# Gathering the first expert groups from unscaled residual rows, with weights in the place of the scaled rows

## What is computed

```python
h = h + mix(rms_norm(h, norm) @ w_in) @ w_out
hf = rms_norm(h, m_norm[layer])
g_idx = argmax(hf @ w_group + b_group)            # one of 4 groups
top_val, top_idx = top_k(e_logits_of_group, 2)    # two of its 8 experts
combine = one_hot(expert_idx) * softmax(top_val) * g_prob
for e in range(32):
    hid = silu(hf @ w_gate[e]) * (hf @ w_up[e])   # 1024 -> 256
    h += (hid @ w_down[e]) * combine[:, e:e + 1]  # 256 -> 1024
```

## Time and profile before

| | before |
|---|---|
| time, median of 3 runs | 781.3 us (780.98 to 781.67) |
| profiled execution, first to last instruction | 778.7 us |
| TensorE matmul busy | 718.9 us (92%) |
| TensorE weight load busy | 459.4 us (59%) |
| DVE busy | 324.4 us (42%) |
| ScalarE busy | 205.9 us (26%) |
| read from HBM | 240.00 MB |
| bytes moved, mean rate | 242.14 MB, 311 GB/s |

### The profile page before, as it was taken

One profiled execution on the slowest core, in us unless ns is written; L12 is line 12 of the kernel. 1 busy time (PEld: TensorE's weight loads), 2 busy tenths in 40 slices (PEclk: granted clock), 3 DMA queues, 4 the chain that ended last, 5 costly groups with the idle time before them and its releaser, 6 DMA issues.

```text
span 778.7 us, 16693 instructions
## 1 busy us (share of the span) xinstructions
PE 718.9 (92%) x7444; PEld 459.4 (59%) x7444; DVE 324.4 (42%) x688; ACT 205.9 (26%) x414; POOL 31.7 (4%) x99
## 2 busy tenths in 40 slices
PE   9999999999989998999999999999998976786696
PEld 7778787658646464564548746884764543343342
DVE  7476977535353422333235065541445321221222
ACT  2574577215100000000041454630510000000003
POOL 7006000000000000000000000000000000000000
PEclk9999999999999997999999999999999998989999
DMA  8644113499999999999999731019999999999995
GB/s 265 201 107 142 56 57 112 161 418 417 386 420 419 420 421 421 417 419 422 411 339 370 231 107 58 2 36 424 421 391 421 422 420 419 421 422 422 420 406 199
DMA packets 72757, 242.14 MB, mean 311 GB/s; under 512 B 9894, under 2 KB 37660, under 8 KB 52588
## 3 DMA queue, kind: packets, MB, share of 16 engines
q1 hardware_dynamic: 72476, 240.52, 79.0%
q10 hardware_dynamic: 208, 0.54, 0.2%
HBM read 240.00 MB, written 1.05 MB: 310 GB/s over the span
## 4 chain that ended last, share of the span: by engine, by line
PE 60%; DMA 15%; DVE 4%; issue 1%; SPq 1%; ACT 0%; ACTq 0%
PE ps L1554 11%; PE ps L1874 10%; PE ps L1396 7%; PE ps L1497 6%; DMA M<-in_m_w_gate_dram 6%; PE ps L1630 5%; PE ps L1512 5%; DMA M<-in_m_w_up_dram 4%; DMA M<-in_m_w_down_dram 4%; PE ps L1035 2%; DVE H L2488 1%; PE ps L1411 1%; PE ps L1696 1%; PE ps L1768 1%; PE ps L1505 1%
## 5 line engine op out<-in xcount | busy, mean ns | idle before, releaser
L1554 PE MATMUL ps<-M 128*32 128x256 f32 x2016 | 124.2, 396 | 18.4 <-DMA M<-in_m_w_gate_dram 11.4
L1554 PEld LDWEIGHTS ps<-M 128*32 128x32 f32 x2016 | 66.7, 114 | 74.7 <-issue 16.9
L1089 PE MATMUL ps<-M 128*128 128x272 f32 x352 | 85.3, 397 | 0.1
L1874 PE MATMUL ps<-M 128*128 128x256 f32 (+2 forms) x288 | 79.9, 434 | 0.0
L1497 PEld LDWEIGHTS ps<-M 128*128 128x128 f32 x608 | 71.5, 192 | 12.3 <-issue 11.8
L1497 PE MATMUL ps<-M 128*128 128x128 f32 x608 | 76.9, 278 | 0.0
L1089 PEld LDWEIGHTS ps<-M 128*128 128x128 f32 x352 | 65.6, 190 | 15.4 <-issue 1.7
L1630 PE MATMUL ps<-M 128*32 128x512 f32 x448 | 58.7, 671 | 15.5 <-DMA M<-in_m_w_down_dram 15.5
L1512 PE MATMUL ps<-M 128*128 128x512 f32 (+1 forms) x120 | 62.8, 647 | 5.3 <-DVE H L2488 5.3
L1874 PEld LDWEIGHTS ps<-M 128*128 128x128 f32 x288 | 53.7, 190 | 22.6 <-issue 15.6
L2485 DVE TENSOR_TENSOR H<-H,ps 128x512 f32<-128x512 f32 x60 | 41.2, 687 | 57.5 <-PE ps L1512 57.3
(11 more groups left out here) (462 smaller groups left out, 843.6 us busy)
## 6 DMA issues: line engine op xcount, KB each, us to landing
M<-in_m_w_gate_dram SPq DMA_DIRECT2D x31, 2048.0 KB, 19.0
M<-in_m_w_down_dram SPq DMA_DIRECT2D x24, 2048.0 KB, 22.8
M<-in_m_w_up_dram SPq DMA_DIRECT2D x24, 2048.0 KB, 21.6
M<-in_o_w_in_dram SPq DMA_DIRECT2D x12, 1024.0 KB, 9.5
M<-in_e_w_in_dram SPq DMA_DIRECT2D x11, 1024.0 KB, 6.7
M<-in_m_w_down_dram SPq DMA_DIRECT2D x10, 1024.0 KB, 18.1
M<-in_m_w_up_dram SPq DMA_DIRECT2D x9, 1024.0 KB, 17.9
M<-in_m_w_down_dram SPq DMA_DIRECT2D x4, 1536.0 KB, 13.3
```

The costliest lines, as they stand in the source:

```text
L1089: ins = pe.matmul(ps[:, n % 4, 0:T], wringE[:, (n // 2) % 4, k, (n % 2) * P:(n % 2) * P + P], (xnE if n else xuE)[:, k], start=(k == 0), s ...
L1554: ins = pe.matmul(ps[32 * e:32 * e + 32, 3 * x, 0:FF], xgT[q % 2][:, k, 32 * e:32 * e + 32], w, start=(k == 0), stop=(k == KD - 1))
L1874: ins = pe.matmul(ps[rows, unit % 4, 0:n], lhs(k), rhs(k), start=(k == 0), stop=(k == KD - 1))
```

## The change

- The two first gathers (q = 0 and q = 1) of layer 0 read the stationary operand straight from `H` (`rows_at`), with a step of eight floats. As these rows are not scaled, `rs` is multiplied into `R` instead: the one-hot matrix goes to `RW[q]`, and `R` is that times `rs`, one more DVE operation each time. `RW` is then weighted in place.
- `normed` is not called before the gather in layer 0, but after `half_done` 1 (tiles 0 and 2) and after the copy of `hidT` in quarter 0 (tile 1). The gather of quarter 2 waits for it, and so does the first `accumulated`, which changes `H`.
- `xn` (1.5 MB) holds the first halves of gate matrices 0 to 2 until then (`first_half`). Their place in slot 1 is free, and the second halves of up matrices 4 to 6 go there without waiting for `half_done`.
- 2 MB of quarter 0 (a down matrix and a half, half an up matrix) are issued after `y_done` 4 and `lru_in` 2, before the wait for `sa_evac`.
- The meta rows' sums in quarters 0 to 5 and in the spare pass of layer 0 are kept in strips: `combine` writes 32 rows in each group of 32 partitions, and one add of 128x256 puts all four pieces into `H[:, 2, 0:256]`. `strips_joined` brings them to the meta rows in quarter 6 (three copies, two adds); the sums of quarter 6 are added in the old form.
- Semaphore counts follow from this (`loaded`, `ld_half`).

```diff
@@ -287,6 +287,7 @@
+        first_half = [[xn[:, n].rearrange("p k t -> p (k t)") for n in range(3)], []]
@@ -357,22 +358,23 @@
-                def whole(u, src):
-                    j = UNIT_SLOT[y][u]
-                    for e in (0, 2):
-                        sp.dma_start(slots[j][:, e:e + 2, :], src[:, e:e + 2, :]).then_inc(s(f"ld_s{j}"), 16)
-                    sp.dma_start(apart[2], src[:, 2, 0:D]).then_inc(s(rest), 16)
+                    sp.wait_ge(s("y_done"), NTURN - 1)
+                    sp.wait_ge(s("lru_in"), 2)
+                    sp.dma_start(slots[3][:, 1, :], down[:, 1, :]).then_inc(s("ld_s3"), 16)
+                    sp.dma_start(slots[3][:, 2, 0:D], down[:, 2, 0:D]).then_inc(s("ld_s3"), 16)
+                    sp.dma_start(apart[2], up[:, 2, 0:D]).then_inc(s("ld_pv_ys"), 16)
-                    whole(2, down[:, 0:4])
+                    sp.dma_start(slots[3][:, 0, :], down[:, 0, :]).then_inc(s("ld_s3"), 16)
+                    sp.dma_start(slots[3][:, 2, D:2 * D], down[:, 2, D:2 * D]).then_inc(s("ld_s3"), 16)
+                    sp.dma_start(slots[3][:, 3, :], down[:, 3, :]).then_inc(s("ld_s3"), 16)
@@ -391,6 +393,10 @@
+                            sp.dma_start(slots[j][:, 0:3, D:2 * D], gate[:, 0:3, D:2 * D]).then_inc(s(f"ld_s{j}"), 16)
+                            sp.dma_start(slots[j][:, 3, :], gate[:, 3, :]).then_inc(s(f"ld_s{j}"), 16)
+                            sp.dma_start(xn.rearrange("p n k t -> p n (k t)"), gate[:, 0:3, 0:D]).then_inc(s(f"ld_s{j}"), 16)
+                            continue
@@ -419,9 +425,9 @@
+                            sp.dma_start(slots[j][:, 0:3, 0:D], up[:, 4:7, D:2 * D]).then_inc(s("ld_half"), 16)
-                            sp.dma_start(slots[j][:, 0:3, 0:D], up[:, 4:7, D:2 * D]).then_inc(s(f"ld_s{j}"), 16)
@@ -806,16 +812,16 @@
-                act.wait_ge(s("rec"), (5, 10)[y])
-                normed(0)
-                if nt == 3:
-                    normed(2)
+                if y == 1:
+                    act.wait_ge(s("rec"), (5, 10)[y])
+                    normed(0)
-                act.wait_ge(s("rec"), (6, 11)[y])
-                normed(1)
+                if y == 1:
+                    act.wait_ge(s("rec"), (6, 11)[y])
+                    normed(1)
@@ -825,6 +831,11 @@
+                    if q == 0 and y == 0:
+                        act.wait_ge(s("half_done"), 2 * y + 1)
+                        act.wait_ge(s("rec"), (6, 11)[y])
+                        normed(0)
+                        normed(2)
@@ -1404,11 +1417,14 @@
+            def rows_at(n, k):
+                return H[:, n, :].rearrange("p (d k) -> p k d", k=KD)[:, k, :]
-                        ins = pe.matmul(ps[:, GATHER_BANK[k // 2], (k % 2) * P:(k % 2) * P + P], xn[:, n, k, :], R[:, n, :],
+                        ins = pe.matmul(ps[:, GATHER_BANK[k // 2], (k % 2) * P:(k % 2) * P + P], rows_at(n, k) if y == 0 else xn[:, n, k, :], R[:, n, :],
...
@@ -1491,10 +1508,11 @@
-                def gather(done=None, ks=range(KD)):
+                def gather(done=None, ks=range(KD), first=False):
-                            ins = pe.matmul(ps[:, 1 + k // 4, (k % 4) * P:(k % 4) * P + P], xn[:, n, k, :], R[:, n, :],
+                            from_rows = rows_at(n, k) if first and y == 0 else xn[:, n, k, :]
+                            ins = pe.matmul(ps[:, 1 + k // 4, (k % 4) * P:(k % 4) * P + P], from_rows, R[:, n, :],
@@ -1511,8 +1529,7 @@
-                        ins = pe.matmul(ps[32 * g:32 * g + META, bank, 0:256], rt_[:, TOK[n]], ys[:, 256 * g:256 * g + 256],
-                                        start=True, stop=True)
+                        ins = pe.matmul(ps[QUAD[g], bank, 0:256], rt_[:, 0:32], ys[:, 256 * g:256 * g + 256], start=True, stop=True)
...
@@ -1549,6 +1571,8 @@
+                            elif u == 0 and k < KD // 2 and e < len(first_half[y]):
+                                w = first_half[y][e][:, FF * k:FF * k + FF]
@@ -1559,7 +1583,8 @@
-                pe.wait_ge(s("xn_set"), (3, 5)[y])
+                if y == 1:
+                    pe.wait_ge(s("xn_set"), (3, 5)[y])
...
@@ -1611,13 +1636,15 @@
-                        gather(ks=range(0, 2))
+                        if y == 0 and q == 1:
+                            pe.wait_ge(s("xn_set"), (3, 5)[y])
+                        gather(ks=range(0, 2), first=(q == 0))
-                        gather(s("g_done"), range(2, 4))
+                        gather(s("g_done"), range(2, 4), q == 0)
@@ -1630,7 +1657,7 @@
-                    gather(ks=range(4, KD)).then_inc(s("g_done"), 1)
+                    gather(ks=range(4, KD), first=(q == 0)).then_inc(s("g_done"), 1)
@@ -2402,9 +2429,14 @@
-                    return tt(R[:, t_].rearrange("p t (e c) -> p t e c", e=4),
-                              iota[:, 1:CAP + 1].unsqueeze(1).unsqueeze(1).to_broadcast([P, m, 4, CAP]),
-                              RM[:, t_, 0:4].unsqueeze(3).to_broadcast([P, m, 4, CAP]), ALU.is_equal).then_inc(s("R_set"), 1)
+                    if y == 1:
+                        return tt(R[:, t_].rearrange("p t (e c) -> p t e c", e=4),
+                                  iota[:, 1:CAP + 1].unsqueeze(1).unsqueeze(1).to_broadcast([P, m, 4, CAP]),
+                                  RM[:, t_, 0:4].unsqueeze(3).to_broadcast([P, m, 4, CAP]), ALU.is_equal).then_inc(s("R_set"), 1)
+                    link(tt(RW[0][:, t_].rearrange("p t (e c) -> p t e c", e=4),
+                            iota[:, 1:CAP + 1].unsqueeze(1).unsqueeze(1).to_broadcast([P, m, 4, CAP]),
+                            RM[:, t_, 0:4].unsqueeze(3).to_broadcast([P, m, 4, CAP]), ALU.is_equal))
+                    tt(R[:, t_], RW[0][:, t_], wide3(rs[:, ri], P, t_, m), ALU.mult).then_inc(s("R_set"), 1)
@@ -2452,12 +2484,17 @@
-                    tt(by_slot(R), iota[:, 1:CAP + 1].unsqueeze(1).unsqueeze(1).to_broadcast([P, nt, 4, CAP]),
-                       RM[:, t_, 4 * q:4 * q + 4].unsqueeze(3).to_broadcast([P, nt, 4, CAP]), ALU.is_equal).then_inc(s("R_set"), 1)
+                    hot = RW[q] if y == 0 and q == 1 else R
+                    made = tt(by_slot(hot), iota[:, 1:CAP + 1].unsqueeze(1).unsqueeze(1).to_broadcast([P, nt, 4, CAP]),
+                              RM[:, t_, 4 * q:4 * q + 4].unsqueeze(3).to_broadcast([P, nt, 4, CAP]), ALU.is_equal)
+                    if hot is not R:
+                        link(made)
+                        made = tt(R[:, t_], hot[:, t_], wide3(rs[:, ri], P), ALU.mult)
+                    made.then_inc(s("R_set"), 1)
-                    tt(by_slot(RW[q % 2]), by_slot(R), WT[:, t_, 4 * q:4 * q + 4].unsqueeze(3).to_broadcast([P, nt, 4, CAP]),
+                    tt(by_slot(RW[q % 2]), by_slot(RW[q] if y == 0 and q < 2 else R), WT[:, t_, 4 * q:4 * q + 4].unsqueeze(3).to_broadcast([P, nt, 4, CAP]),
@@ -2483,15 +2520,31 @@
-                    for g in range(4):
-                        c = slice(256 * g, 256 * g + 256)
-                        ins = tt(H[0:META, 2, c], H[0:META, 2, c], ps[32 * g:32 * g + META, 6 + j % 2, 0:256], ALU.add)
-                    return ins
+                    return tt(H[:, 2, 0:256], H[:, 2, 0:256], ps[:, 6 + j % 2, 0:256], ALU.add)
+                    if y == 0 and q == 0:
+                        v.wait_ge(s("xn_set"), (3, 5)[y])
+                        if y == 0 and j == 0 and q == NQ - 2:
+                            for g in range(4):
+                                c = slice(256 * g, 256 * g + 256)
+                                ins = tt(H[0:META, 2, c], H[0:META, 2, c], ps[32 * g:32 * g + META, 6, 0:256], ALU.add)
+                            ins.then_inc(s("acc"), 1)
+                            continue
+                def strips_joined():
+                    strip_rows = (at(36608, 2, 256), at(28800, 1, 256))
+                    v.wait_ge(s("acc"), acc0 + nu * (NQ - 2))
+                    for g in range(1, 4):
+                        last = v.tensor_copy(strip_rows[(g - 1) // 2][0:META, (g - 1) % 2], H[32 * g:32 * g + META, 2, 0:256])
+                    link(last)
+                    for x, c in zip(strip_rows, (slice(256, 768), slice(768, D))):
+                        last = tt(H[0:META, 2, c], H[0:META, 2, c], x[0:META].rearrange("p g c -> p (g c)"), ALU.add)
+                    link(last)
@@ -2539,6 +2592,8 @@
+                    if q == NQ - 2 and y == 0:
+                        strips_joined()
```

18 lines of the change are left out of this document (12 added, 6 removed).

## The result

The changed kernel takes 792.78 us, the median of its runs (792.37 to 793.58), beside 781.48 for the kernel before on the same chip: a ratio of 1.014, 95% interval 1.012 to 1.016. It is 11.3 us slower, where 5.6 was forecast. The profiled execution has a span of 791.1 us, 12.4 more than before, and at the last down product of the first expert stage TensorE is 12.16 us late already. So the whole loss lies ahead of that point.

What follows compares the result with a forecast made beforehand. TensorE and the transfers were taken to end the first expert stage together, with TensorE deciding after the change: +10.4 + 0.5 - 5.3 = +5.6 us on 781.3 gives 786.9 us. Range 777.9 to 789.2, likeliest case 785 to 789.

Steps and rivals of the forecast that it cites:

- What bounds the kernel: First expert stage: TensorE and transfers finish together, each less than 1 us from holding up the other.
- The early transfers: 2 MB issued in SyncE's idle time after 127.0 us: cost nothing, pull the transfers' end forward by at most 5.0 us.
- The strided loads: First two gathers, 96 weight loads with a 32-byte step: spacing 226 ns instead of 118, +10.4 us on TensorE.
- Rivals 1 and 2: Strided loads are free: 778.4 us, chance 0.20; the step costs a third of the forecast price: 780 us, chance 0.08.
- The one-hot multiply: One more DVE operation of 128x256 ahead of the first gather, multiplying rs into R: +0.5 us.
- The normalising copies: Three ScalarE copies moved behind the half gate product: no gain, no cost; 2 us once if their cover were gone.
- The strips: Meta rows added in one DVE operation instead of four: all seven TensorE waits go, -5.3 us.
- The buffers: 1.5 MB of slot 1 free earlier, then the queue waits for TensorE's late releases: a lull at 197 to 209 us.
- rival 3: Spare pass: the clock stays up instead of falling to 0.50 from 303 us; transfers decide, 783.9 us, chance 0.16.
- Rival 4: Strided gathers: the clock falls since matmuls fill only half the time, another 4.0 us, 790.9 us, chance 0.06.

Runs made afterwards that it cites:

- f6: Kernel before with only the meta rows' sums in strips added: 781.94 us, ratio 1.0006.
- g4: f6 with 1.75 MB less to transfer, one second half of a gate matrix cut to an eighth: 777.91 us, ratio 0.9945.
- e3: Changed kernel with the two first gathers reading 128 adjacent floats, so other columns than the computation wants: 787.73 us, ratio 1.007.
- e4: Changed kernel with adjacent loads in the two first gathers and the 2 MB not sent ahead: 781.24 us, ratio 0.9985.
- f7: Kernel before with only the 2 MB sent ahead added, as three DMAs: 785.96 us, ratio 1.0058.
- e1: Changed kernel with the 2 MB not sent ahead but behind the wait for sa_evac: 789.28 us, ratio 1.008.
- g3: Changed kernel with adjacent loads in the two first gathers and the early 2 MB in four pieces of 512 KB: 784.41 us, ratio 1.0014.

## Where the prediction was right and where it failed

- **What bounds the kernel.** "A gain needs both to become faster; one of them slower is enough for a loss" held: f6 and g4 show the first half, e3 against e4 the second. The sum then didn't stay with it. It let TensorE decide and counted the strips' 5.3 us in full.
- **The early transfers: "they cost nothing".** This is the step that failed: a term put at nothing that measured 4.5 us alone (f7), 3.5 to 4.4 in the changed kernel (e1). I asked whether SyncE's queue was free, and DMA was, but not who else uses the DMA engines in that time: the instruction queue stands on the same page, with 59 packets. The stall and the lower clock behind it make TensorE 4.6 us later than the 0.3 that it was late already. In f7 it is 3.4 us later by them, and 1.6 more come from the fall of the clock in the first gather.
- **The strided loads.** Right in kind, and too small for TensorE: 335 ns for 305, and a pair every 243 ns (23.3 us of loads for 96) for 226. Before it was 118 (11.3 us), so the term is +12.0 in place of +10.4 us. In the time it isn't worth that much, since the transfers stand between: 5.1 us (e3) to 8.0 (e1 less e4). The forecast carried all of it into the end of the stage. Twice the columns' part, 222 ns, was taken from ScalarE and from the transposing load at a step of two; the ordinary load at a step of two pays 4 ns, at eight 143. The bound of 11.3 us came from the same wrong row and was too low as well. Rivals 1 and 2 are out.
- **The one-hot multiply**: +0.42 us, where 0.5 was forecast. The normalising copies cost nothing, as said.
- **The strips.** All seven waits went and TensorE got 0.76 us a quarter, as said. In the time they are worth 0 (f6, in the kernel before; the changed kernel wasn't run without them), for TensorE waits for weights instead. So -5.3 is the second wrong term. The errors partly cancel, which is luck: the step was counted 2.4 to 5.3 us too dear in time, the strips 5.3 too good, the early block 3.5 to 4.5 too cheap.
- **The buffers.** The lull came where it was forecast, and deeper. Half the gate product released its slot 9.5 us later than before (204.56 against 195.06), where 4.3 was forecast; 4.9 of it is the late start. In the stretches of the change and of the kernel before:

```profile
190.00:214.00 24.00, 22.78 (x205) 18.71 (x204) 12.44 (x48) 9.04 (x13) 0.00 (x0) 0.93 0.72 256
214.00:230.00 16.00, 16.00 (x101) 12.78 (x105) 2.08 (x3) 3.10 (x4) 0.00 (x0) 1.00 0.99 366
230.00:380.00 150.00, 144.83 (x1447) 85.98 (x1440) 49.68 (x96) 11.55 (x27) 0.53 (x1) 0.99 1.01 417
```

```profile
194.00:214.00 20.00, 19.93 (x252) 13.60 (x248) 6.86 (x21) 3.45 (x7) 0.00 (x0) 1.00 1.00 385
```

  To 420 GB/s the change lacks 9.4 and 2.1 us in the first two stretches, and 1.1 from 160 to 190 us (405); before it was 1.7 and 0.3. That is +10.6 us. The weights' issue begins 4.9 us later (151.52 for 146.62), 5.0 us of bytes are there already, and the rest of the stage runs at 417 for 419 to 420 (+1.1): together +11.6, against 12.16 measured. The prediction's same account ended at +4.7, without the late start and with releases 5 us too early. (Its rival 3 puts the transfers at +2.9 and the time at 783.9; 781.3 + 2.9 is 784.2.)
- **Rival 3** was half right: the clock stayed up longer and was at half from 320.1 to 323.5 us, 3.4 us in place of 10.2. The six products after the wait ran at full speed, 2.46 us less than in the earlier trace rows. By the account above it didn't show in the time, since the transfers decided; no run takes it out alone. Rival 4's fall came as well (0.50 from 193.8 to 197.2 us), and cost nothing there: a pair takes 244 ns at either clock. But its cause was not the strided load: the same fall comes with adjacent ones in e3, g3 and f7, and there it costs 1.6 us.

TensorE's own account is less exact: 16.85 us at the second quarter, less 5.3 and 2.46, and 4.6 of waits for DMA, give 13.7 where 12.16 were measured. About 1.5 us of it I can't place.

## What to carry to other kernels

Before a transfer is called free, look at the page's other queues: 2 MB of weights held back an instruction fetch, TensorE stood for 2.3 us and a low clock followed; with pieces of 512 KB and gaps between them TensorE stood for 0.3 to 0.9 us and no low clock followed in that part. Where a stage ends with its transfers, count for each edit when buffers come free, and not what an engine saves; starting earlier only fills the same room earlier. To find which of the two decides, take work away from one and bytes from the other: here 5.3 us of work were worth 0, and 4.2 us of bytes on top of them 4.0.
